# A state-space scan that gets its rows of running sums by DMA and masks them on GpSimd, not by matmuls

## The reference

```python
def step(state, inp):
    x_c, a_c, B_c, C_c = inp
    cum = jnp.cumsum(a_c, axis=1)                      # a = dt * A, per head
    cum_t = jnp.moveaxis(cum, 1, -1)
    seg = cum_t[..., :, None] - cum_t[..., None, :]
    decay = jnp.exp(jnp.where(causal, seg, -jnp.inf))
    cb = jnp.einsum('bign,bjgn->bgij', C_c, B_c)
    y_intra = jnp.einsum('bgij,bghij,bjghp->bighp', cb, decay, x_c)
    ...
```

## Time and profile before

| what | value |
|---|---|
| median of three runs | 1592.39 us |
| span of the profiled execution | 1590.5 us |
| TensorE busy, weight loads busy | 98%, 95% |
| VectorE, ScalarE, GpSimd busy | 62%, 49%, 11% |
| chain that ended last | TensorE 90%, VectorE 6%, ScalarE 2%, DMA 1%, issue 1% |
| the scan | from 238 to about 369 us of the span |
| transfers | 289.67 MB, mean 182 GB/s; GpSimd's queue 3.88 MB of it |

### The profile page before, as it was taken

One profiled execution on the slowest core, in us unless ns is written; L12 is line 12 of the kernel. 1 busy time (PEld: TensorE's weight loads), 2 busy tenths in 40 slices (PEclk: granted clock), 3 DMA queues, 4 the chain that ended last, 5 costly groups with the idle time before them and its releaser, 6 DMA issues.

```text
span 1590.5 us, 30228 instructions
## 1 busy us (share of the span) xinstructions
PE 1555.8 (98%) x12541; PEld 1509.4 (95%) x12541; DVE 988.8 (62%) x1277; ACT 773.8 (49%) x1021; POOL 174.5 (11%) x137
## 2 busy tenths in 40 slices
PE   8999999989999999999999999999999999999997
PEld 5999998879999999999999899999999999899997
DVE  5887994345776555555475775555655558765545
ACT  3555565554455434544453654443544435554433
POOL 0300003333100010000022020001300013030001
PEclk9999999999999999999999999999999999999999
DMA  8976763324545554555545335555455454455550
GB/s 327 361 288 218 286 232 113 107 80 143 202 170 186 185 184 153 203 184 184 184 142 200 134 117 194 183 185 185 154 186 183 184 186 133 160 185 185 185 186 27
DMA packets 42185, 289.67 MB, mean 182 GB/s; under 512 B 4875, under 2 KB 7051, under 8 KB 7532
## 3 DMA queue, kind: packets, MB, share of 16 engines
q1 hardware_dynamic: 41244, 284.44, 49.7%
q0 software_dynamic: 848, 3.88, 0.6%
HBM read 285.15 MB, written 3.15 MB: 181 GB/s over the span
## 4 chain that ended last, share of the span: by engine, by line
PE 90%; DVE 6%; ACT 2%; DMA 1%; issue 1%; SPq 0%; ACTq 0%; DVEq 0%
PE banks L628 20%; PE banks L631 20%; PE banks L630 20%; PE banks L756 6%; PE banks L759 6%; PE banks L758 6%; DVE w_lo L1665 2%; DMA raw<-in_panels 1%; DVE XS L1813 1%; PE banks L640 1%; PE banks L645 1%; PE banks L642 1%; ACT w_hi L1206 1%; DVE H L1821 1%; PE banks L1002 1%
## 5 line engine op out<-in xcount | busy, mean ns | idle before, releaser
L1665 DVE TENSOR_TENSOR w_lo<-raw,w_hi 128x1024 fp32r<-128x1024 f32 x490 | 613.2, 1260 | 480.1 <-ACT w_hi L1206 474.8
L1206 ACT ACTIVATE w_hi<-raw 128x1024 fp32r<-128x1024 f32 x490 | 515.2, 1057 | 569.7 <-PE banks L631 405.1
L628 PE MATMUL banks<-H,w_lo 128*128 128x256 f32 x1696 | 477.7, 282 | 2.9 <-DVE w_lo L1665 1.9
L631 PE MATMUL banks<-H,w_hi 128*128 128x256 f32 x1696 | 477.3, 281 | 0.0
L630 PE MATMUL banks<-H,w_hi 128*128 128x256 f32 x1696 | 477.2, 281 | 0.0
L628 PEld LDWEIGHTS banks<-H,w_lo 128*128 128x128 f32 x1696 | 319.2, 188 | 3.8 <-DVE w_lo L1665 2.5
L630 PEld LDWEIGHTS banks<-H,w_hi 128*128 128x128 f32 x1696 | 319.2, 188 | 0.0
L631 PEld LDWEIGHTS banks<-H,w_hi 128*128 128x128 f32 x1696 | 319.2, 188 | 0.0
L631 PE MATMUL banks<-HH,w_hi 128*128 128x256 f32 x960 | 270.1, 281 | 0.0
L630 PE MATMUL banks<-HH,w_hi 128*128 128x256 f32 x960 | 270.1, 281 | 0.0
L628 PE MATMUL banks<-HH,w_lo 128*128 128x256 f32 x960 | 270.1, 281 | 0.0
(11 more groups left out here) (296 smaller groups left out, 1904.5 us busy)
## 6 DMA issues: line engine op xcount, KB each, us to landing
raw<-in_panels SPq DMA_DIRECT2D x269, 1024.0 KB, 4.8
bias_rows<-rev POOLq DMA_DIRECT2D x1, 2048.0 KB, 15.7
XS<-in_x_t SPq DMA_DIRECT2D x1, 1024.0 KB, 6.6
near<-bias_rows POOLq DMA_DIRECT2D x8, 128.0 KB, 3.4
out_t<-XS SPq DMA_DIRECT2D x4, 256.0 KB, 2.6
ws<-in_ws_t POOLq DMA_DIRECT2D x1, 512.0 KB, 8.8
cols<-in_cols SPq DMA_DIRECT2D x1, 180.0 KB, 2.5
wdt<-in_wdt POOLq DMA_DIRECT2D x1, 128.0 KB, 3.8
```

The source lines that it names most:

```text
L628: pe.matmul(acc, w_lo[:, panel_slot, at:at + P], operand[:, kk, 0, :], start=starts and c == chunks[0], stop=False)
L631: return pe.matmul(acc, w_hi[:, panel_slot, at:at + P], operand[:, kk, 0, :], start=False, stop=stops and c == chunks[-1])
L1206: act.activation(w_hi[:, sl, w], raw[:, r, w], ACT.Copy).then_inc(panel_hi, 1)
L1665: vec.tensor_tensor(w_lo[:, sl, w], raw[:, r, w], w_hi[:, sl, w], ALU.subtract).then_inc(panel_lo, 1)
```

## The change

TensorE no longer builds the rows. The running sums with heads on the partitions are made once, in partitions 0 to 31, and their blocks are laid out anew: second-chunk sums first, then the first chunk's, then the second's again, so that for each head the two blocks that need a mask lie side by side. ScalarE copies them to `cum_row` in f32; GpSimd stores that to a DRAM buffer `cum_rows` (32 x 384 values, 48 KB). For each pair GpSimd issues one DMA that reads the pair's two rows (3 KB) and writes them to all 128 partitions of one of two slots of `rows` (384 KB written), and masks the diagonal blocks of both heads with two `affine_select` of 128x256. ScalarE's exponentials read the slot in SBUF instead of banks 5 and 6. A slot is filled again after the exponentials that read it; the select of pair n+1 stands at the head of GpSimd's turn n, ahead of the gating of block n-2; the DMA of pair n+2 stands ahead of the multiply of pair n. The stores and the first two DMAs come before the loop. `cum_r`, `pick_r`, their operations and semaphores are gone; `never` stays, as other matmuls use it. `tri`, `heads`, `ea` and `wdt_r` now share their space with `rows`.

```diff
+ROW_SLOTS = 2
...
+        cum_row = sb("cum_row", [32, 3 * P], F32, phase)
...
+        rows = sb("rows", [P, ROW_SLOTS, 6 * P], F32, phase)
...
+            def rows_in(n):
+
+                pair = cum_rows[2 * n:2 * n + 2, :].rearrange("(o h) t -> o (h t)", o=1)
+                pool.dma_start(rows[:, n % ROW_SLOTS, :], pair.to_broadcast([P, 6 * P])).then_inc(rows_landed[n % ROW_SLOTS], 16)
+
+            def rows_causal(n):
+                pool.wait_ge(rows_landed[n % ROW_SLOTS], 16 * (n // ROW_SLOTS) + 16)
+                for r in range(2):
+                    diagonal = rows[:, n % ROW_SLOTS, 3 * P * r:3 * P * r + T].rearrange("p (a i) -> p a i", a=2)
+                    pool.affine_select(out=diagonal, in_=diagonal, compare_op=ALU.is_ge, fill=MASKED, base=0,
+                                       pattern=[[0, 2], [1, P]], channel_multiplier=-1).then_inc(S["rows_masked"], 1)
+
+            pool.wait_ge(S["cum_copied"], 1)
+            pool.dma_start(cum_rows, cum_row[:, :]).then_inc(S["cum_stored"], 16)
+            pool.wait_ge(S["cum_stored"], 16)
+            for n in range(ROW_SLOTS):
+                rows_in(n)
+            rows_causal(0)
             for n in range(PAIRS):
+                if n + 1 < PAIRS:
+                    rows_causal(n + 1)
                 if n >= 2:
                     gating(n - 2)
                 pool.wait_ge(S["exp_done"], 4 * (n + 1))
+                if n + ROW_SLOTS < PAIRS:
+                    rows_in(n + ROW_SLOTS)
                 pool.wait_ge(S["cb_copied"], n // 2 + 1)
...
-                for rows in (slice(0, 32), slice(32, 64)):
-                    pe.matmul(banks[rows, 6, 0:P], a_v[:, 0, :], tri[:, :], start=True, stop=True)
-                    second = banks[rows, 6, P:3 * P].rearrange("q (a i) -> q a i", a=2)
-                    pe.matmul(second, a_v[:, 0, :], ones[:, :].unsqueeze(1).to_broadcast([P, 2, P]), start=True, stop=False)
-                    last = pe.matmul(second, a_v[:, 1, :], tri[:, :].unsqueeze(1).to_broadcast([P, 2, P]),
-                                     start=False, stop=True)
-                last.then_inc(S["cum_done"], 1)
+                pe.matmul(banks[0:32, 6, P:2 * P], a_v[:, 0, :], tri[:, :], start=True, stop=True)
+                second = banks[0:32, 6, 0:3 * P].rearrange("q (a i) -> q a i", a=3)[:, 0:3:2, :]
+                pe.matmul(second, a_v[:, 0, :], ones[:, :].unsqueeze(1).to_broadcast([P, 2, P]), start=True, stop=False)
+                pe.matmul(second, a_v[:, 1, :], tri[:, :].unsqueeze(1).to_broadcast([P, 2, P]),
+                          start=False, stop=True).then_inc(S["cum_done"], 1)
...
-                decay_rows(n)
...
-                    act.activation(cum_r[:, :], banks[0:64, 6, 0:3 * P], ACT.Copy).then_inc(S["cum_hi"], 1)
+                    act.activation(cum_row[:, :], banks[0:32, 6, 0:3 * P], ACT.Copy).then_inc(S["cum_copied"], 1)
...
             def decays(n):
-                act.wait_ge(S["row_done"], n + 1)
+                act.wait_ge(S["rows_masked"], 2 * (n + 1))
+                if n < 2:
+                    act.wait_ge(S["silu_done"], SSM_GROUPS - 1 + n)
                 if n >= 2:
                     act.wait_ge(S["y_done"], n - 1)
                 for r in range(2):
                     h = 2 * n + r
-                    for t, (at, size) in enumerate(((0, T), (T, P))):
-
+                    for t, (at, size, row) in enumerate(((0, T, P), (T, P, 0))):
+                        row += 3 * P * r
                         act.activation(decay(n)[:, 3 * P * r + at:3 * P * r + at + size],
-                                       banks[:, 5 + r, at:at + size], ACT.Exp,
+                                       rows[:, n % ROW_SLOTS, row:row + size], ACT.Exp,
                                        bias=dtv[:, 4, t, h:h + 1]).then_inc(S["exp_done"], 1)
...
-            vec.tensor_tensor(pick_r[:, :], ident[0:64, 0:32], ident[0:64, 32:64], ALU.add).then_inc(S["pick_set"], 1)
...
-                vec.wait_ge(S["cum_hi"], 1)
-                vec.tensor_tensor(cum_r[32:64, :], banks[32:64, 6, 0:3 * P], cum_r[32:64, :], ALU.subtract)\
-                    .then_inc(S["cum_lo"], 1)
```

More of the change, by code:

```diff
@@ L180, in two_blocks @@
 def two_blocks(nc, panels, x_in, c_in, cols_in, heads_in, ws_in, bs_in, wdt_in, rel_in, onehot_in, inv_in,
-               skew, out):
+               skew, cum_rows, out):
     ctx = ExitStack()
@@ L241, in two_blocks @@
         xbc = sb("xbc", [P, 32, T], F32, phase)
-        tri = sb("tri", [P, P], F32, phase)
-        heads = sb("heads", [P, 2, 32], F32, phase)
         c_r = sb("c_r", [P, KD, COPY], F32, phase)
         cb = sb("cb", [P, 2, 3 * P], F32, phase)
-        wdt_r = sb("wdt_r", [P, KD, 2, 32], F32R, phase)
         dtv = sb("dtv", [P, 5, TT, 32], F32, phase)
-        ea = sb("ea", [P, 32], F32, phase)
-        cum_r = sb("cum_r", [64, 3 * P], F32R, phase)
-        pick_r = sb("pick_r", [64, 32], F32R, phase)
+        cum_row = sb("cum_row", [32, 3 * P], F32, phase)
+        before_scan = ExitStack()
+        tri = sb("tri", [P, P], F32, before_scan)
+        heads = sb("heads", [P, 2, 32], F32, before_scan)
+        ea = sb("ea", [P, 32], F32, before_scan)
+        wdt_r = sb("wdt_r", [P, KD, 2, 32], F32R, before_scan)
+        before_scan.close()
+        rows = sb("rows", [P, ROW_SLOTS, 6 * P], F32, phase)
         phase.close()
@@ L287, in two_blocks @@
         loaded = [sem(f"panel_loaded_{r}") for r in range(RAW)]
+        rows_landed = [sem(f"rows_landed_{r}") for r in range(ROW_SLOTS)]
         panel_hi, panel_lo, half_used = sem("panel_hi"), sem("panel_lo"), sem("half_used")
@@ L302, in two_blocks @@
             "sgu_vn sgu_vt sgu_vcopy sgu_mix sgu_y sgu_hi sgu_lo ws_masked "
-            "wdt_hi wdt_lo dt_raw dt_y dt_exp dt_one dt_ln dt_ea dt_a pick_set bs_clear bs_rounded bs_split y_log cum_done cum_got cum_hi cum_lo "
-            "cb_done cb_copied xt_done xdt_done row_done exp_done never_set m_done y_done y_skip "
+            "wdt_hi wdt_lo dt_raw dt_y dt_exp dt_one dt_ln dt_ea dt_a bs_clear bs_rounded bs_split y_log cum_done cum_got cum_copied cum_stored rows_masked "
+            "cb_done cb_copied xt_done xdt_done exp_done never_set m_done y_done y_skip "
             "y_gated y_sq y_sums y_var y_root y_f y_hi y_lo "
@@ L993, in scores_and_tokens @@
                 last.then_inc(S["xt_done"], 1)
-            def decay_rows(n):
-                for r in range(2):
-                    if n:
-                        pe.wait_ge(S["exp_done"], 4 * (n - 1) + 2 * (r + 1))
-                    h = 2 * n + r
-                    pick = pick_r[:, h:h + 1].to_broadcast([64, P])
-                    pe.matmul(banks[:, 5 + r, 0:3 * P], pick, cum_r[:, :], start=True, stop=False)
-                    diagonal = banks[:, 5 + r, :].rearrange("p (a i) -> p a i", i=P)[:, 0:3:2, :]
-                    last = pe.matmul(diagonal, ident_r[:, :], never[:, :].unsqueeze(1).to_broadcast([P, 2, P]),
-                                     start=False, stop=True)
-                last.then_inc(S["row_done"], 1)
             def head_outputs(n):
@@ L1030, in group_sums @@
                 last.then_inc(S["y_sums"], 1)
-            pe.wait_ge(S["cum_lo"], 1)
+            pe.wait_ge(S["cum_copied"], 1)
             pe.wait_ge(S["cum_got"], 1)
@@ L1035, in _ @@
             pe.wait_ge(S["never_set"], 1)
-            pe.wait_ge(S["pick_set"], 1)
             pe.wait_ge(S["mod_taken"], 12)
@@ L2368 @@
     args.append(nc.dram_tensor("bias_rows", (P, HEADS * BIAS_COLS), F32).ap())
+    args.append(nc.dram_tensor("cum_rows", (SSM_HEADS, 3 * P), F32).ap())
     args.append(nc.dram_tensor("out_t", (P, KD, T), F32, kind="ExternalOutput").ap())
```

## The result

The changed kernel takes 1597.3 us (median of 7 runs, 1595.6 to 1598.4), the kernel before 1592.2 us (median of 7, 1591.4 to 1594.1). The ratio is 1.0036, with a 95% interval of 1.0025 to 1.0046. The forecast was a gain of 0.5 us, and the time moved the other way. The profiled execution of the changed kernel took 1598.4 us with a span of 1596.6, 6.1 us more than the 1590.5 of before. It is the slowest of the seven, 1.1 us above their median, so sums read from its trace come out near 6 us where the medians differ by 5.1.

A forecast was written before the change was run, and what follows sets the result against it. TensorE is busy 98%, but its row matmuls cover an almost equally long chain over the other engines. 3.0 + 0 - 1.2 - 0.6 - 1.2 + 0.5 = 0.5 us gained, 1591.9 us; 8 in 10: 1586 to 1600.

The forecast's parts named there:

- the end: Turns 11 to 15: rows covered, gain 0; later multiplies and selects -0.6 us, one more slow clock stretch -1.2 us.
- the start: Turns 0 to 2: despite two landings in sequence, the gate's bank is free when it was before; gain 0.
- selects to 252.7: Start: pair 2's rows issued 247.9, landed 251.9, then two selects, 0.84 us a pair, done at 252.7.
- the middle: Turns 3 to 10: four odd turns gain 4.2 us, multiply meeting low part takes 1.2; +3.0 us (1.8 to 4.2).
- running sums: Making of the running sums: products of the second row group go, +0.5 us (0 to 0.7).
- clock behind the bank: Start: TensorE idles before the gate's bank, then one more slow clock stretch, -1.2 us (0 to -2).
- Rival 1: Scan: the rows' matmul time comes off whole, 1572 us; chance 3%.
- Rival 2: Scan: same mechanism without side costs, low part and multiply unhurt, clock holds; 1586 to 1589 us; chance 25%.
- Rival 3: Scan: the transfer's landing ends last; 1596.5 us at a 5.7 us landing, 1606 at 6.5; chance 18%.
- Rival 4: Middle: the clock falls there too, three turns at 1.5 us each, 1596.4 us; chance 12%.
- Rival 5: Odd turns: shared port at full price, 0.6 us a turn, 1593.1 us; 42% together with the forecast.
- The signs set out beforehand: Group sums await square, scores variance; two turns 13.7 to 14.3 us; selects 4.8 us after issue; bank free 260 to 261.

The follow-up runs named there:

- experiment 1: Changed kernel without the row transfers and selects, slots filled once with the mask value; 1587.9 us, ratio 0.9974 to the kernel before.
- rows_static: The run of experiment 1: changed kernel without row transfers and selects, slots filled once with the mask value; 1587.9 us.
- Experiment 2: Changed kernel with selects of 128x4 instead of 128x256, transfers and issues as they were; 1596.5 us, ratio 1.0029 to the kernel before.
- experiment 6: Changed kernel with the transfers of pairs 2 to 15 issued on ScalarE's queue instead of GpSimd's; 1590.5 us, ratio 0.9995 to the kernel before.
- keep_busy: Changed kernel with matmuls of no use to the result put where TensorE waits; 1595.4 us, ratio 1.0023 to the kernel before.
- issue_behind_multiply: Changed kernel with GpSimd issuing each transfer behind the multiply of its turn instead of ahead; 1596.7 us, ratio 1.0039 to the kernel before.
- issue_on_act: The run of experiment 6: changed kernel with the transfers of pairs 2 to 15 issued on ScalarE's queue; 1590.5 us.

## Why the prediction was wrong, by its own steps

Three terms failed. The largest is the end, booked at -1.8 us and measured at -4.8: its clock at -1.2 is -1.9 to -3.8, its collisions at -0.6 are the rest. Then the start, booked at 0 and measured at -1.7, by the step "selects to 252.7". Then the middle, by the price of a low part beside a multiply, 0.3 us a turn in the forecast and 0.8 measured. Behind the last two and part of the first stands one mechanism that was priced too low: VectorE's low part and GpSimd's operations shut each other out. The terms in us gained, forecast and as the marks of the two profiled executions give them:

| term | forecast | measured | read from |
|---|---|---|---|
| running sums | +0.5 | +0.3 | first scores, 237.60 against 237.86 |
| start | 0 | -1.7 | bank free, 262.23 against 260.82, less the line above |
| clock behind the bank | -1.2 | -1.2 | outputs of pair 1, 265.09 against 262.45 |
| middle | +3.0 | +1.4 | scores of turn 10, 316.62 against 315.38 |
| end | -1.8 | -4.8 | last group sums, 380.73 against 374.70 |
| sum | +0.5 | -6.0 | |

**What bounds the kernel, and the gain of the rows: right.** The chain skip, gating, square, rounding, low part, variance is what came late next, and without GpSimd's new work two turns take 13.93 us where 13.9 was forecast (experiment 1). (14.87 - 1.05 is 13.8; rows_static's low parts still meet the multiply for 0.3 us and take 1.37 to 1.43.)

**The middle: right mechanism, mis-sized price.** The forecast let multiply and low part collide and took 0.3 us for it, between bounds of 0 and 0.6. It was 0.8 to 1.0: 2.00 to 2.22 us against 1.23 in the four turns; from rows_static to the changed kernel the pitch grows from 13.93 to 14.76. The upper bound was itself too low. It came from a low part of 1.70 whose overlap with a multiply was 0.6 us, and I took that price for the ceiling although I had worked out an overlap of 0.9 us (267.6 to 268.5). A price per us of overlap would have been right: (1.70 - 1.23) / 0.62 = 0.76 from the row of before, and (2.04 - 1.23) / 0.95 = 0.85 from the one of after. The price rises because nearly all of the overlap is lost: the low part ends 1.09 us after the multiply does, so its time is 1.23 + overlap - 0.14. From 255 to 375 us of the 14 traces 68 low parts start under a multiply that has 0.2 us or more to go, and this fits 63 of them to 0.02 us; in the other five the low half follows the multiply, and the low part ends 1.09 us after that. For an overlap of 0.9 it gives 0.8. Four turns at 0.8 make 3.2 instead of the 1.2 that the forecast took, so +1.0, near the +1.4 measured.

**Start: wrong by 1.7 us, through the selects.** The landings were as forecast: 3.9 us in the median (forecast 4.0), 3.7 at 248.08 and 4.6 at 254.27. The step that failed is "selects to 252.7", where the selects were given 0.84 us. At 251.80 they stood beside VectorE's low parts, and took 2.52 us. The earlier trace rows had shown VectorE busy for all of 249.5 to 251, just ahead of it. Everything behind slid with them: the next issue (254.27 where 252.7 was forecast), the next landing, gating, square, eviction, and the bank (262.23 where 260.8 was). I had priced the collision for the multiply and not for the new instructions themselves. Experiment 2 shows that a smaller select would have helped by less than 1 us, experiment 6 that an issue which doesn't stand behind the selects does.

**Clock: right in size at the start, wrong at the end.** One slow stretch behind the gate's bank was forecast at 1.2 us and cost 1.2. At the end 1.2 us was taken, bounds 0 and 3. The profiled execution has a granted clock of 0.68 from 326 to 342, and keep_busy puts the cost at 1.9 to 3.4 us, or 3.8 from turn 11 on (50.12 against 46.36). GpSimd's new work isn't needed for it, since rows_static has it too. (A small slip: 278.13 - 270.41 less two halves is 2.0, not 1.9. It changes nothing.)

**End: the collision again, beside the clock.** Of 4.8 us lost there the clock has 1.9 to 3.8. The rest, 1 to 3 us, goes to the collision: the low part of turn 11 took 2.52 us against 1.70, that of turn 13 took 3.25 against 1.43 in the kernel before. In its queue the two scalings and the variance follow, and from its start to the variance's it is 4.26 us (352.13 to 356.39) against 3.16 before (347.23 to 350.39); in turn 11 it is 3.56 (331.49 to 335.05) against 2.60 (330.08 to 332.68). The forecast had 0.6 us for "multiplies and selects beside the norm work".

**The rivals.** Rival 1 fell, with TensorE's time down 14 us and the total up. Rival 2, no side costs at 1586 to 1589 us, is where rows_static is (1587.9). Rival 3 gave a time close to the measured one (1596.5), but by another mechanism: the landings were on time, and in the middle they end last only in issue_behind_multiply. Rival 4, the clock in the middle, fell: 278 to 326 is at 1.00 throughout. Rival 5, the port at full price, was right and priced too low, and I kept it inside the forecast instead of giving it the start and the end too. The same cause in three places (0.8 us or more in each odd turn, 1.7 us at the selects, 1.0 and 1.1 us in turns 11 and 13) was priced in one.

**The signs set out beforehand.** Group sums waited some 0.3 us behind the square, and scores were released by the variance, as said. But two turns took 14.76 us and not 13.7 to 14.3, the selects were done 6.24 us after the issue (248.08 to 254.32) and not 4.8, and the bank came free at 262.23 and not by 261.

## What to carry to other kernels

When work moves from TensorE to GpSimd, don't ask only whether GpSimd has room; lay each of its instructions, the DMA issues too, over VectorE's two-input operations as they will stand after the change, and price each us of overlap at 0.8 us of VectorE's or more, the new instructions' own delay included. When an edit takes cover from a chain, look for what in that chain needn't be in front: here an operation of 0.4 us stood behind one of 1.2 us that no one on the path waited for, and its place was free before the change and worth 5 us after it. A change that measures slower can be the better base: with two moves of order its version takes 1583 us, and the matmuls it removed are then worth some 6 us instead of 3.

## What the runs showed of the hardware

- VectorE's low part (128x1024, two inputs in SBUF) and GpSimd shut each other out. The one that starts second waits. A select pair of 128x4 took 0.34 us alone and 2.18 beside low parts; one of 128x256 0.77 and 2.52. VectorE pays too: 1.23 us becomes 1.86 with 0.77 us of overlap with a multiply and 2.04 with 0.95. A multiply of 128x768 that starts ahead of the low part stays at 1.81 to 1.86 us; one that starts behind takes 2.68 (251.44 in the kernel before). The Trainium skill, GPSIMD Engine Reference, Specifications, names contention with VectorE's instructions that have two SBUF inputs, and the trace agrees; the price is from these rows.
- A transfer of 384 KB that repeats one line over 128 partitions takes 3.9 us from issue to landing on GpSimd's queue (3.4 to 7.3) and 4.0 on ScalarE's (3.2 to 5.9, in issue_on_act). For GpSimd's queue the Trainium skill, DMA: Bandwidth & Descriptors, Anatomy of one DMA, would make it an estimate of 2.9 us; the trace doesn't agree.
- Issuing it took 0.58 us on GpSimd and 0.33 us on ScalarE, whose next operation starts 0.46 us after the last exponential (251.82 in issue_on_act). On ScalarE's queue it was the better place all the same, because nothing in a collision stood behind it.
- Matmuls of no use held the granted clock at 1.00 (2.4 GHz) from 326 to 374 us, where TensorE had idled 1.5 to 3.8 us at a time and the clock had been as low as 0.68 on average, a good part of the stretch at the lower level. Holding it gave 1.9 us by the medians, of some 3.4 us that the slow matmuls had shown there. That the next waits took up the rest, since other engines end them, was argued and not shown.
